# Writing TensorE's four MLP group iterations as a hardware loop instead of four copies

## The chip, the cores and the metric

The kernel runs on one core of a Trainium2 chip. The metric is the device time of one execution in microseconds (us), lower is better. The kernel before takes 1731.78 us (median of three runs, 1730.12 to 1737.38).

## The reference, cut to what matters

One inference step of a two-layer decoder trunk, with weights shared by a prompt of 512 tokens and 8 samples of one token (520 columns in all). Each layer has a mixer (differential attention with gated linear attention in layer 0, a recurrent block in layer 1), and then a squared-ReLU MLP:

```python
def sq_relu_mlp(h, w_up, w_down):
    return jnp.square(jax.nn.relu(h @ w_up)) @ w_down
...
yp = yp + rmsnorm(sq_relu_mlp(rmsnorm(yp, g[2]), w_up[layer], w_down[layer]), g[3])
```

The model width is 1024 and the MLP's inner width is 4096. The change touches only how the MLP's products are issued.

## The kernel before

All activations lie transposed: 8 tiles of 128 features by 520 tokens. Every product is done in two parts: the activation and the weight are each split into a high and a low part, and three products (high by high, low by high, high by low) are summed in PSUM. Weights arrive in chunks of 1024 rows by 256 columns (1 MB). SyncE loads a chunk into `RAW` (two slots), ScalarE copies it to `W_hi` (L699), VectorE makes `W_lo` (L1044), and TensorE multiplies it in `products` (L1525). A chunk gives two output tiles; a tile is 8 steps of 3 products by 2 halves of 260 columns, so 48 matmuls, and a chunk is 96 matmuls with as many weight loads.

The MLP of a layer is 32 chunks in four groups of eight: in a group, chunks 0 to 3 give 8 tiles of the inner layer from `H_hi`/`H_lo`, which VectorE and ScalarE turn into `U_hi`/`U_lo` (L1391, L909, L1394, L1396), and chunks 4 to 7 multiply these by the down weights, and VectorE adds the results into `ACC` (L1401). SyncE, ScalarE and VectorE already run the four groups as a hardware loop (`Fori`, at L544, L899 and L1383). TensorE's program has the four groups written out one after the other by a Python loop, in layer 0 and again in layer 1.

The engines run in order and are coupled by counting semaphores. In the MLP TensorE waits for:

- `w_lo_ready`, once per chunk (L1527), for the split weights;
- `banks_free`, once per tile (L1531), for the PSUM banks of the tile two before;
- `h_ready`, eight times in chunk 0 of a group, through `set_ready` (L1563), with the same constants in each group;
- `u_lo_ready`, eight times in chunk 4 of a group (L1575).

The values come from the class `Chunk`, which adds `g * per_group` to a constant. Where `g` is a Python integer the value is a constant in the program. Where `g` is the loop's variable, the value is in a register, worked out by register instructions on the engine that waits:

```python
at = lambda value, per_group: value if g is None else g * per_group + value
self.ready = at(c + 1, 8)
...
self.banks_free = [at(m // 2, 8) for m in self.tiles]
```

Of the kernel before, what the change touches and what calls it, by code (L numbers as in the profile page):

```python
# [114 lines left out]
def trunk(nc, ctx, a, o):  # L115
# [171 lines left out]
    def sem(name):  # L287
        return ctx.enter_context(nc.semaphore(name))
# [126 lines left out]
    u_lo_ready = sem("u_lo_ready")  # L415
# [1073 lines left out]
    def _(pe):  # L1489
# [35 lines left out]
        def products(ch, hi, lo, ready=None, after=None, together=False):  # L1525

            pe.wait_ge(w_lo_ready, ch.ready)  # L1527

            def free(i):
                if ch.tiles[i] >= 2:  # L1530
                    pe.wait_ge(banks_free[ch.par[i]], ch.banks_free[i])  # L1531

            def step(i, k):
                cols = slice(P * i, P * i + P)
                for n, (w, x) in enumerate(((W_hi, hi), (W_hi, lo), (W_lo, hi))):
                    for j, half in enumerate(halves):
                        t = MM_(PS[:, 2 * ch.par[i] + j, 0:HALF], w[:, ch.slot, k, cols], x[:, k, half],  # L1537
                                start=k == 0 and n == 0, stop=k == KT - 1 and n == 2)
                if k == KT - 1:
                    t.then_inc(tiles_done, 1)  # L1540

            if together:
                for i in range(ch.count):
                    free(i)
                for k in range(KT):
                    ready(k)
                    for i in range(ch.count):
                        step(i, k)
                if after:
                    for i in range(ch.count):  # L1550
                        after(i)
            else:
                for i in range(ch.count):
                    free(i)
                    for k in range(KT):
                        if ready and i == 0:
                            ready(k)
                        step(i, k)
                    if after:
                        after(i)  # L1560

        def set_ready(m):
            return lambda k: pe.wait_ge(h_ready, 8 * m + k + 1)  # L1563
# [3 lines left out]
                products(Chunk(c0 + j), H_hi, H_lo, set_ready(m) if j == 0 else None)  # L1567

        def mlp(layer, c0, m):
            for g in range(4):  # L1570
                for j in range(4):
                    products(Chunk(c0 + j, g), H_hi, H_lo, set_ready(m) if j == 0 else None)
                for j in range(4, 8):
                    products(Chunk(c0 + j, g), U_hi, U_lo,
                             (lambda k, g=g: pe.wait_ge(u_lo_ready, g * 8 + (32 * layer + k + 1))) if j == 4 else None)  # L1575

        sum_squares(0)

# [200 lines left out]
        sum_squares(1)  # L1779
        sum_squares(2)  # L1780
        mlp(0, C_MLP0, 2)
        sum_squares(3)
        sum_squares(4)
# [36 lines left out]
        sum_squares(5)  # L1820
        sum_squares(6)
        mlp(1, C_MLP1, 5)
        sum_squares(7)

# [53 lines left out]
```

## Time and profile before

| | |
|---|---|
| median of three runs | 1731.78 us (1730.12 to 1737.38) |
| the profiled execution: its time | 1731.78 us |
| the profiled execution: first to last instruction | 1729.9 us |
| TensorE matmuls, busy | 1494.3 us, 86% |
| VectorE, ScalarE, GpSimd, busy | 56%, 28%, 21% |
| mean granted TensorE clock | 0.893 of full speed |
| TensorE instructions | 10,928 matmuls and as many weight loads |

The profile names engines PE (TensorE's matmuls), PEld (its weight loads, which overlap the matmuls), DVE (VectorE), ACT (ScalarE), POOL (GpSimd) and SP (SyncE). A q behind a name (PEldq, ACTq, DVEq) means the engine's sequencer, that is a semaphore, register or branch instruction, which is not counted as busy time. PEclk is the granted TensorE clock. DMA queues named "instruction" carry the engines' own programs; queue q1 carries the weights.

### The profile page before, as it was taken

To read this page: it belongs to the slowest core of one execution; us is meant where nothing else is said; L and a number is where in the kernel's file an instruction comes from. 1 tells how busy PE (TensorE), PEld (TensorE's weight loads), DVE (VectorE), ACT (ScalarE), POOL (GpSimd) and SP (SyncE) were. 2 spreads that over 40 slices of the span, in tenths; PEclk is the share of its full clock that TensorE was granted. 3 is DMA by queue.
4 is the path that set the end of the run, shared out by engine and by line. 5 is a ranking of instruction groups with operands and counts; after the bars stand their busy time and mean duration, and the time that the engine had idled before them with its cause. 6 is when DMAs were issued, how large, how long until landed. Compare 5 with 4: busy or idle time off the path is not lost.

```text
span 1729.9 us, 25378 instructions
## 1 busy us (share of the span) xinstructions
PE 1494.3 (86%) x10928; PEld 1328.3 (77%) x10928; DVE 960.5 (56%) x1104; ACT 477.2 (28%) x701; POOL 358.0 (21%) x237
## 2 busy tenths in 40 slices
PE   4999636678987679799999999699897999999995
PEld 3999613346662139699999999589896999999994
DVE  3498867668866842743535353667827435343533
ACT  3322423322113112421212122346424212121222
POOL 0185756557536200200000000100302000000001
PEclk8999856768768659999999999899998999999998
DMA  8387766669668642023222332021220332233221
GB/s 285 122 302 258 257 241 239 244 245 385 243 246 348 286 147 73 27 96 98 96 83 90 98 97 84 16 75 54 94 75 25 98 98 77 95 98 98 76 71 50
DMA packets 128260, 250.54 MB, mean 145 GB/s; under 512 B 5255, under 2 KB 108699, under 8 KB 111508
## 3 DMA queue, kind: packets, MB, share of 16 engines
q0 software_dynamic: 18432, 134.23, 20.5%
q1 hardware_dynamic: 100292, 104.21, 18.8%
q10 hardware_dynamic: 9432, 10.55, 1.9%
q8 instruction: 86, 1.41, 0.3%
q14 instruction: 18, 0.15, 0.0%
HBM read 241.30 MB, written 7.73 MB: 144 GB/s over the span
## 4 chain that ended last, share of the span: by engine, by line
PE 72%; DVE 15%; ACT 5%; DMA 3%; issue 2%; SPq 2%; POOL 1%; ACTq 0%; POOLq 0%; DVEq 0%
PE PS L1537 59%; PE PS L1522 3%; PE PS L1756 2%; DVE TMP L1079 2%; DVE HRS L1312 2%; DMA SBIAS<-bias_scratch 1%; SPq L521 1%; DVE RS L1053 1%; PE PS L1669 1%; PE PS L1689 1%; DVE ST L1290 1%; PE PS L1659 1%; DVE SC L1095 1%; PE PS L1711 1%; PE PS L1795 1%
## 5 line engine op out<-in xcount | busy, mean ns | idle before, releaser
L1537 PE MATMUL PS<-H_hi,W_hi 128*128 128x260 f32 x1936 | 397.3, 287 | 23.2 <-DVE H_lo L1049 13.2
L1537 PE MATMUL PS<-H_hi,W_lo 128*128 128x260 f32 x1936 | 393.7, 285 | 0.0
L1537 PE MATMUL PS<-H_lo,W_hi 128*128 128x260 f32 x1936 | 393.5, 285 | 0.0
L1537 PEld LDWEIGHTS PS<-H_hi,W_hi 128*128 128x128 f32 x1936 | 303.9, 191 | 26.3 <-issue 19.1
L1537 PEld LDWEIGHTS PS<-H_lo,W_hi 128*128 128x128 f32 x1936 | 302.3, 191 | 0.0
L1537 PEld LDWEIGHTS PS<-H_hi,W_lo 128*128 128x128 f32 x1936 | 302.3, 191 | 0.0
L1044 DVE TENSOR_TENSOR W_lo<-RAW,W_hi 128x2048 fp32r<-128x2048 f32 x94 | 216.5, 2303 | 133.3 <-ACT W_hi L699 132.6
L699 ACT ACTIVATE W_hi<-RAW 128x2048 fp32r<-128x2048 f32 x94 | 179.5, 1909 | 278.1 <-PE PS L1537 277.7
L625 POOL TENSOR_TENSOR X<-X,TMP 128x520 f32<-128x520 f32 x16 | 26.7, 1667 | 956.9 <-DVE TMP L1079 956.9
L1537 PE MATMUL PS<-U_hi,W_lo 128*128 128x260 f32 x1024 | 206.4, 283 | 0.0
L1537 PE MATMUL PS<-U_lo,W_hi 128*128 128x260 f32 x1024 | 206.0, 283 | 0.0
L1537 PE MATMUL PS<-U_hi,W_hi 128*128 128x260 f32 x1024 | 206.0, 282 | 0.0
L578 POOL TENSOR_TENSOR PROD<-KV,QB 128x1024 f32<-128x1024 f32 x64 | 152.1, 2376 | 105.6 <-DVE SC L1095 75.1
L1537 PEld LDWEIGHTS PS<-U_hi,W_hi 128*128 128x128 f32 x1024 | 157.9, 188 | 0.0
L1537 PEld LDWEIGHTS PS<-U_hi,W_lo 128*128 128x128 f32 x1024 | 157.9, 188 | 0.0
L1537 PEld LDWEIGHTS PS<-U_lo,W_hi 128*128 128x128 f32 x1024 | 157.4, 188 | 0.0
L1401 DVE TENSOR_TENSOR ACC<-ACC,PS 128x520 f32<-128x520 f32 x64 | 44.6, 697 | 200.3 <-PE PS L1537 200.3
L909 ACT ACTIVATE UF<-SQ 128x520 f32<-128x520 f32 x64 | 40.9, 639 | 279.9 <-DVE SQ L1391 279.9
L1391 DVE SCALAR_TENSOR_TENSOR SQ<-PS,RS 128x520 f32<-128x520 f32 x64 | 44.8, 700 | 112.8 <-PE PS L1537 112.8
L1522 PE MATMUL PS<-SQ,ONES 128*128 128x260 f32 x256 | 76.0, 456 | 35.4 <-ACT SQ L721 35.4
L1689 PE MATMUL PS<-KV,PM 128*32 128x512 f32 x512 | 92.7, 821 | 8.9 <-DMA KV<-in_cache_v,CIDX 8.2
L1522 PEld LDWEIGHTS PS<-SQ,ONES 128*128 128x128 f32 x256 | 54.2, 226 | 56.0 <-issue 28.1
(284 smaller groups left out, 1612.7 us busy)
## 6 DMA issues: line engine op xcount, KB each, us to landing
RAW<-in_w_up SPq DMA_DIRECT2D x32, 1024.0 KB, 5.4
RAW<-in_w_down SPq DMA_DIRECT2D x32, 1024.0 KB, 5.1
RAW<-in_w_in_even SPq DMA_DIRECT2D x13, 1024.0 KB, 7.9
RAW<-in_w_in_odd SPq DMA_DIRECT2D x8, 1024.0 KB, 5.5
RAW<-in_w_out_odd SPq DMA_DIRECT2D x5, 1024.0 KB, 5.2
RAW<-in_w_out_even SPq DMA_DIRECT2D x4, 1024.0 KB, 6.2
x_saved<-X ACTq DMA_DIRECT2D x1, 2080.0 KB, 6.4
X<-x_saved SPq DMA_DIRECT2D x1, 2080.0 KB, 7.7
```

Source lines behind the costliest of these rows:

```text
L578: nc.gpsimd.tensor_tensor(PROD[:, 1], KV[i % RING][:, 2:4, :], QB[:, None, n // 32, :].to_broadcast([P, 2, 512]), ALU.mult).then_inc(prod1 ...
L699: A(W_hi[:, ch.slot], RAW[:, ch.slot], ACT.Copy).then_inc(w_hi_ready, 1)
L909: A(UF[:, i], RL[:, i], ACT.Square).then_inc(uf_ready, 1)
L1044: V.tensor_tensor(W_lo[:, ch.slot], RAW[:, ch.slot], W_hi[:, ch.slot].bitcast(F32), ALU.subtract).then_inc(w_lo_ready, 1)
L1079: t = V.scalar_tensor_tensor(TMP[:, q], ACC[:, kt + q], VEC[:, gain + kt + q:gain + kt + q + 1], RS[:, 1], ALU.mult, ALU.mult)
L1312: link(V.reciprocal(HRS[:, q % 2], HRS[:, q % 2]))
L1391: V.scalar_tensor_tensor(pair(RL[:, i]), banks(ch.par[i]), 0.0, pair(RS[:, 1]), ALU.max, ALU.mult).then_inc(banks_free[ch.par[i]], 1)
L1401: V.tensor_tensor(pair(ACC[:, m]), pair(ACC[:, m]), banks(ch.par[i]), ALU.add).then_inc(banks_free[ch.par[i]], 1)
L1522: t = MM_(PS[:, 4 + i, 0:HALF], ONES[:], SQ[:, kt % 2, half], start=kt == 0, stop=kt == KT - 1)
L1537: t = MM_(PS[:, 2 * ch.par[i] + j, 0:HALF], w[:, ch.slot, k, cols], x[:, k, half], start=k == 0 and n == 0, stop=k == KT - 1 and n == 2)
L1689: t = MM_(PS[32 * pos:32 * pos + 32, 6, :], PM[:, (n // 4) % 2, 4 * (n % 4) + pos].rearrange("p b j -> p (b j)"), KV[i % RING][:, pos, :], ...
L1756: t = MM_(out[:, GLA_CHUNK * n:GLA_CHUNK * n + GLA_CHUNK], ST[rows, hp, n], QE[rows, hp, P * tb + GLA_CHUNK * n:P * tb + GLA_CHUNK * (n + ...
```

## The change

`mlp` in TensorE's program runs its four groups as a hardware loop. The body is in the program once per layer and is run four times. The semaphore values that depend on the group are now held in registers.

```diff
         def mlp(layer, c0, m):
-            for g in range(4):
+            with pe.Fori(0, 4) as g:
                 for j in range(4):
                     products(Chunk(c0 + j, g), H_hi, H_lo, set_ready(m) if j == 0 else None)
                 for j in range(4, 8):
                     products(Chunk(c0 + j, g), U_hi, U_lo,
-                             (lambda k, g=g: pe.wait_ge(u_lo_ready, g * 8 + (32 * layer + k + 1))) if j == 4 else None)
+                             (lambda k: pe.wait_ge(u_lo_ready, g * 8 + (32 * layer + k + 1))) if j == 4 else None)
```

## Rows read from the trace of the kernel before

**Rows 1.** The page: busy time of each engine, share of span, instructions.
```profile
span 1729.9 us, 25378 instructions
## 1 busy us (share of the span) xinstructions
PE 1494.3 (86%) x10928; PEld 1328.3 (77%) x10928; DVE 960.5 (56%) x1104; ACT 477.2 (28%) x701; POOL 358.0 (21%) x237
```

**Rows 2.** The chain that ended last: start, length (us), what.
```profile
716.61 369.05 PE PS L1537 x3072
...
1324.67 369.07 PE PS L1537 x3072
```

**Rows 3.** Windows of layer 0's four groups: busy time (instructions), clock, DMA.
```profile
core 0: us, PE busy (x) PEld busy (x) DVE busy (x) ACT busy (x) POOL busy (x), PEclk, DMA share, GB/s
716.61:808.80 92.19, 92.19 (x769) 92.19 (x769) 41.26 (x41) 20.60 (x17) 1.02 (x1) 1.00 0.29 92
808.80:901.05 92.25, 92.25 (x770) 92.25 (x769) 38.57 (x40) 20.02 (x16) 0.00 (x0) 1.00 0.29 92
...
sum 369.04, PE 369.04 PEld 369.04 DVE 156.96 ACT 81.72 POOL 1.02; mean PE 92.26 PEld 92.26 DVE 39.24 ACT 20.43 POOL 0.26
```

**Rows 4.** Waits, 718 to 1084 us: who waited for whom, us, times, longest.
```profile
ACT UF L909 <- DVE SQ L1391: 139.9, 32, 5.1
ACT W_hi L699 <- PE PS L1537: 138.9, 15, 9.6
```

**Rows 5.** DMA queues, whole span, then 716 to 1086 us: packets, MB, share.
```profile
q8 instruction: 86, 1.41, 0.3%
q14 instruction: 18, 0.15, 0.0%
...
q8 instruction: 25, 0.41, 0.5%
q14 instruction: 2, 0.02, 0.0%
```

**Rows 6.** TensorE's semaphore instructions at L1563, 805 to 809 us.
```profile
L1563 PEldq EVENT_SEMAPHORE  x1: 51/51/51, 806.6 to 806.6; - x1
```

**Rows 7.** Timeline around 808.5 us: where the second group's matmuls begin.
```profile
808.45 0.40 PE L1537 MATMUL PS<-U_hi,W_lo 128*128 128x260 f32 x2
808.57 0.19 PEld L1537 LDWEIGHTS PS<-H_hi,W_hi 128*128 128x128 f32 x1
```

**Rows 8.** TensorE's semaphore instructions at L1563, 40 to 43 us.
```profile
L1563 PEldq EVENT_SEMAPHORE  x1: 51/51/51, 41.8 to 41.8; - x1
```

**Rows 9.** DMA queues, 42.85 to 43 us.
```profile
DMA packets 1, 0.02 MB, mean 109 GB/s; under 512 B 0, under 2 KB 0, under 8 KB 0
## 3 DMA queue, kind: packets, MB, share of 16 engines
q8 instruction: 1, 0.02, 38.8%
```

**Rows 10.** ScalarE's sequencer at its loop's end, 797 to 798 us (L899, L698).
```profile
L899 ACTq ALU_OP  x1: 35/35/35, 797.4 to 797.4; - x1
L899 ACTq COMPARE_BRANCH  x1: 67/67/67, 797.4 to 797.4; - x1
L899 ACTq FUSED_REGOPS  x1: 50/50/50, 797.6 to 797.6; - x1
...
L698 ACTq FUSED_REGOPS  x1: 37/37/37, 797.7 to 797.7; - x1
```

**Rows 11.** VectorE's sequencer at its loop (L1383), whole span.
```profile
L1383 DVEq ALU_OP  x8: 40/40/40, 808.9 to 1693.8; - x8
L1383 DVEq COMPARE_BRANCH  x8: 50/56/67, 809.0 to 1693.9; - x8
```

**Rows 12.** Timeline of VectorE: the last `U_lo` of a group, a `W_lo`.
```profile
764.71 0.70 DVE L1396 TENSOR_TENSOR U_lo<-UF,U_hi 128x520 fp32r<-128x520 f32 x1
...
810.84 2.29 DVE L1044 TENSOR_TENSOR W_lo<-RAW,W_hi 128x2048 fp32r<-128x2048 f32 x1 [1.25 <-ACT W_hi L699]
```

## The prediction, made before the changed kernel ran

> **What bounds the kernel now.** I read the page's busy times first: TensorE is busy for 1494.3 of 1729.9 us, the other engines for 56% or less [rows 1]. Then the chain of work that ended last: each layer's MLP is one unbroken piece of TensorE's matmuls, 369.05 us at 716.61 and 369.07 us at 1324.67, 3072 matmuls each [rows 2]. Together they are 738.1 us, 43% of the span, and they are all that the change touches. The windows of the four groups of layer 0 show TensorE busy for 92.19 of 92.19 us and 92.25 of 92.25 us, at granted clock 1.00 (the 2.4 GHz level) [rows 3]. Divided out, 369.05 / 3072 = 0.120 us for one weight load and matmul. In the list of waits of that stretch TensorE does not occur at all: the longest entries are ScalarE waiting for VectorE and for TensorE [rows 4]. So there is nothing in these stretches that the change could give back: no gap, full clock, the same 3072 matmuls after as before. Any effect is a cost, and the question is whether it is covered.
>
> **The change, part by part.**
>
> *What it removes.* Three of four copies of the body per layer, from TensorE's program. In layer 0's MLP, instruction queue q8 moves 25 packets, 0.41 MB, which over four groups is 6.2 packets or 0.10 MB per group; over the span q8 moves 86 packets and 1.41 MB [rows 5]. 10,928 matmuls and 10,928 weight loads [rows 1] in 1.41 MB come to 64.5 bytes each, so q8 carries TensorE's program, and a packet holds about 256 instructions. That traffic is 0.5% of the DMA engines' time in the stretch [rows 5], and TensorE never waits in it. Removing it is worth nothing.
>
> *What it adds inside the body.* Per group 32 waits get a value from a register: 8 for `w_lo_ready`, 16 for `banks_free`, 8 for `u_lo_ready`. The `h_ready` ones keep their constants. The trace of before shows no register instruction on TensorE. The nearest rows are ScalarE's, 35 to 50 ns [rows 10], and VectorE's, 40 ns [rows 11]. At 50 ns for each of 32, that is 1.6 us of sequencer time per group, spread over 92 us, and never more than three in a row (0.15 us). The cover is the sequencer's lead over the array. The semaphore instruction in front of the second group is done at 806.6 [rows 6], while the weight load behind it starts at 808.57 [rows 7]: the sequencer is 2.0 us ahead, some 17 pairs at 0.120. So 0.15 us hides. The bounds are 0 and, if nothing covers it, 8 groups x 1.6 = 13 us. I take 0, since the lead is thirteen times the longest burst.
>
> Nor does a wait that now stands in a register come due sooner. The last `U_lo` of a group ends at 764.71 + 0.70 = 765.4 [rows 12]. Its step is the eighth of the chunk that begins at 716.61 + 46.1 = 762.7, so it is due at 762.7 + 7 x 0.72 = 767.8, and 2.4 us are left. A `W_lo` made from 810.84 to 813.1 [rows 12] is for the chunk due at 808.6 + 11.5 = 820.1, with 7 us left. Behind a waiting instruction on TensorE stands only TensorE's own stream; VectorE and ScalarE wait for its tiles, and with no delay there they keep their times.
>
> *What it adds at the loop's end.* Three taken branches per layer, six in all. (The last pass falls through, and the first is entered in line.) A back-edge has a part inside the sequencer. ScalarE's loop shows it: its closing register instruction at 797.4, the branch 67 ns, and the last register instruction of the next pass's first wait at 797.7 [rows 10]. I take 0.4 us from first to last.
>
> The second part is the code. The loop's start lies 6.2 packets back, and whether it is still in the engine's instruction memory no row shows. The loops of VectorE and ScalarE took six such branches each with only 2 q14 packets in the whole stretch [rows 5], but their bodies are short: VectorE's has some 40 instructions and as many register and semaphore ones. So I bound it. The lower bound is 0: the code is there, and the 0.4 us lies inside the lead of 2.0. For the upper, the price of one fetch is read where TensorE's sequencer had been standing at a wait: its semaphore instruction is released at 41.8 [rows 8], and the next code packet runs inside 42.85 to 43.0 and on; it is alone there, filling 38.8% of 16 engines x 0.15 us = 0.93 us [rows 9]. From the release to the packet's end that is 42.9 + 0.93 - 41.8 = 2.0 us, and 2.5 when a packet takes 1.4 (25 packets at 0.5% of 16 x 370 us average 1.2). One fetch then leaves 0.4 + 2.0 to 2.5 - 2.0 = 0.4 to 0.9 us of idle array per back-edge, 2.4 to 5.4 us for six. Two fetches one after the other leave 2.4 to 3.4 us, 14 to 20 us for six. I take one fetch, at 0.65 us: 6 x 0.65 = 4 us. VectorE, ScalarE and SyncE then simply run that much later, since they wait for TensorE's tiles [rows 4].
>
> The Trainium skill has a rule on this, in "Runtime: NRT & Kernel Launch", section on instruction fetch mechanics: fetch is sequential, and a taken branch to a target outside a window of two 16 KB pages stalls until that page is fetched. That speaks against the change, and by it all six back-edges pay. The size of the code packets here agrees (1.41 MB / 86 = 16 KB). No trace so far shows a far branch.
>
> *Sum.* 0 (traffic) + 0 (registers) + 4 (six back-edges) = +4 us. Against the profiled execution, 1731.78 us with a span of 1729.9 and 1.9 around it, that is 1736; its time is also the median of the runs, so no correction is needed.
>
> **The rivals.** About 0.5% (8.7 us) is what a measurement of this kernel tells from no change.
>
> 1. *The body stays in the engine.* Then nothing is fetched at a back-edge, and 0.4 us is inside the lead of 2.0: 1732 us. For it: a memory of eight packets would hold the body's 6.2, and VectorE's and ScalarE's loops show no refetch [rows 5]. Against: q8's packets come one by one all through the unrolled stretch, so nothing shows more than the next one being kept. q8 would fall to about 86 - 6 x 6.2 = 49 packets. The Trainium skill has a rule for this too: "Advanced Engine Details and Errata", section on the ISA cache, gives TensorE 128 KB where the others have 32 KB, yet also says there are only two lines of 16 KB; by the first figure the body fits, by the second it does not.
>
> 2. *The stall is long.* A branch out of line costs more than a fetch in line: it starts with nothing in flight, or the packet behind the target is needed before it has come, or the packet queues behind weight traffic. It decides from 8.7 / 6 + 2.0 = 3.45 us per back-edge on: slower by more than 0.5%. With two fetches in a row (0.4 + 4.0 to 5.0 us) it is 14 to 20 us, and in between, with 3.5 to 4.4 us per back-edge, 9 to 14: 1741 to 1752 us. For it: nothing suggests that target and next packet come together. Against: with an empty lead the array still needs 256 x 0.06 = 15 us for a packet's instructions, so a second fetch hides unless the loop starts close to a packet's end.
>
> 3. *Register instructions are dear on TensorE.* If they had to wait until the array has drained, each of the 32 sites per group would lose the lead. At even 0.2 us each that is 8 x 32 x 0.2 = 51 us, 1783 us. Against: TensorE's semaphore instructions (51 ns) run 2.0 us ahead of the array, so the sequencer does not wait for it there [rows 6, 7].
>
> 4. *Faster.* No mechanism gives it: there is no idle time to remove [rows 3].
>
> **How the numbers follow.** My forecast (a fetch at each back-edge, 1 to 8.7 us in all) has 0.37, centred on 1736. Rival 1 has 0.30 (1732). Rival 2 has 0.26 (1741 to 1752). Rival 3 has 0.04. Faster by over 0.5% has 0.03, from noise alone. So: slower 0.26 + 0.04 = 0.30, same 0.37 + 0.30 = 0.67, faster 0.03. For the range, rival 1 less the lower spread of the runs (1732 - 2) gives about 1729, and the upper end cuts rival 2 at 2.4 us per back-edge, 1732 + 14 = 1746. What is left out is rival 3, the dear end of rival 2, and noise, under 2 in 10. The forecast's own range is 1732 to 1740.
>
> **What would show each step.** In the changed kernel's windows, TensorE should be busy without a gap inside a group at 0.120 us a pair; gaps of tens of ns at each tile would show rival 3. At the group boundaries near 808.8, 901 and 993 us there should be an idle of 0.4 to 0.9 us in the forecast, none in rival 1, over 1.5 us in rival 2. The granted clock should stay at 1.00 through them, since the array was busy until then. q8's count tells fetch from no fetch: if the body is fetched anew each pass it stays at 86 or rises by up to a packet or two per pass (86 to 98); if it stays, it falls to about 49. The prediction is wrong if the MLP stretches grow by more than 4.4 us each, or if another stage moves: the rest of TensorE's program is untouched, but its packets' boundaries shift.

## The result: 25 us slower, and all of it in one of the two loops

The changed kernel takes 1756.29 us (median of four, 1755.25 to 1759.3) against 1730.95 for the kernel before; the ratio is 1.0144, 95% interval 1.0113 to 1.0175. The forecast was 1736 us with a range of 1729 to 1746. The profiled execution took 1753.37 us, with a span of 1751.6: 21.7 us more than the profiled execution of before, and these 21.7 are what the traces below account for.

The page of the changed kernel: busy times hardly moved, the clock's mean neither, and q8 moves fewer code packets than before [rows 1, 5].

```profile
span 1751.6 us, 25540 instructions
## 1 busy us (share of the span) xinstructions
PE 1492.6 (85%) x10928; PEld 1326.9 (76%) x10928; DVE 960.4 (55%) x1104; ACT 476.5 (27%) x701; POOL 357.9 (20%) x237
...
q8 instruction: 77, 1.26, 0.3%
```

The chain that ended last answers to [rows 2] (start, length, what):

```profile
717.77 92.26 PE PS L1537 x768
...
815.35 94.78 PE PS L1537 x768
...
915.46 94.27 PE PS L1537 x768
...
1014.59 94.01 PE PS L1537 x768
...
1346.33 369.03 PE PS L1537 x3072
```

Layer 1 is still one unbroken piece of 369.03 us. Layer 0 has fallen into its four passes. Between the first and the second lie 815.35 - (717.77 + 92.26) = 5.3 us, then 5.3 and 4.9: 15.5 us of idle array. And the passes behind a gap are longer than the first, by 2.5, 2.0 and 1.8 us, 6.3 together. 15.5 + 6.3 = 21.8 us, the whole loss.

The windows around the first back-edge show what the 2.5 us are (columns as in [rows 3]):

```profile
807.60:809.90 2.30, 2.30 (x21) 2.21 (x19) 0.00 (x0) 0.00 (x0) 0.00 (x0) 1.00 0.09 20
809.90:815.30 5.40, 0.12 (x2) 0.00 (x0) 2.99 (x2) 1.91 (x1) 0.00 (x0) 0.84 0.01 3
815.30:820.30 5.00, 4.96 (x23) 4.99 (x24) 0.00 (x0) 0.00 (x0) 0.00 (x0) 0.50 0.68 213
820.30:830.00 9.70, 9.70 (x82) 9.70 (x82) 2.42 (x4) 0.64 (x1) 0.00 (x0) 0.99 0.00 0
```

In the 5 us behind the gap the granted clock is 0.50, the 1.2 GHz level, and 23 matmuls run where 42 fit at 0.120 us. Before the gap it was 1.00, and the fall came inside the gap (0.84 on average there).

TensorE's sequencer at the closing branch (L1570), whole span, then between 807 and 816 us, then the first register instruction of the next pass (L1531):

```profile
L1570 PEldq COMPARE_BRANCH  x8: 76/226/4115, 807.8 to 1713.2; - x8
...
L1570 PEldq COMPARE_BRANCH  x1: 4115/4115/4115, 807.8 to 807.8; - x1
L1570 PEldq FUSED_REGOPS  x1: 52/52/52, 812.0 to 812.0; - x1
...
L1531 PEldq ALU_OP  x1: 36/36/36, 815.1 to 815.1; - x1
```

The branch itself takes 4115 ns at 807.8. Then one register instruction runs at 812.0, and the next one in the program only at 815.1. So there are two stalls in a row, 4.1 and 3.1 us, and the array, which had 2 us of work queued, is idle from 809.9 to 815.3. The idle time is put down to no releaser:

```profile
815.31 0.50 PEld L1537 LDWEIGHTS PS<-H_hi,W_hi 128*128 128x128 f32 x2 [5.50 <-issue]
```

The code queue shows what was waited for. The rows are of 717 to 1109 us (layer 0's MLP), of 808.5 to 908.5 (one pass), of 808.5 to 811, of 811.9 to 814, and of 1345.9 to 1715 (layer 1's):

```profile
q8 instruction: 34, 0.56, 0.6%
...
q8 instruction: 9, 0.15, 0.7%
...
q8 instruction: 1, 0.02, 4.3%
...
q8 instruction: 1, 0.02, 2.8%
...
q8 instruction: 7, 0.11, 0.1%
```

Layer 0's stage fetches 34 packets where it fetched 25 before [rows 5]: seven in the first pass and nine in each pass that follows a back-edge, one of them in each of the two stalls. Layer 1's fetches seven in the whole stage, none between its first back-edge and its exit. One loop is fetched anew on each pass, the other is kept in the engine and costs nothing. Their bodies have the same length and the same instructions.

One more packet belongs to the picture. It starts just before the branch does (807.7 to 807.8 us; the branch starts at 807.83), so while the target was still to be reached, the engine had asked for one packet more:

```profile
q8 instruction: 1, 0.02, 64.8%
```

### The profile page after: what moved, and what is told of

Read it like the earlier page. It is cut to its first block, busy times and chain, and to the rows that moved or that the text cites. A ratio compares the mean times of both kernels' runs of the same rounds, so it can differ in the third digit from the quotient of the medians.

```text
span 1751.6 us, 25540 instructions
## 1 busy us (share of the span) xinstructions
PE 1492.6 (85%) x10928; PEld 1326.9 (76%) x10928; DVE 960.4 (55%) x1104; ACT 476.5 (27%) x701; POOL 357.9 (20%) x237
## 4 chain that ended last, share of the span: by engine, by line
PE 72%; DVE 15%; ACT 5%; DMA 3%; issue 2%; SPq 2%; POOL 1%; ACTq 0%; POOLq 0%; DVEq 0%
PE PS L1537 59%; PE PS L1522 3%; PE PS L1756 2%; DMA SBIAS<-bias_scratch 2%; DVE HRS L1312 2%; SPq L521 1%; PE PS L1689 1%; DVE RS L1053 1%; DVE TMP L1079 1%; PE PS L1669 1%; DVE SC L1095 1%; PE PS L1659 1%; PE PS L1795 1%; PE PS L1711 1%; DVE ST L1290 1%
```

## The experiments

The theory I formed from this (A): TensorE's instruction memory keeps eight packets of 16 KB (256 instructions), gives up the oldest for a new one, and asks for the next packet on entering one. The body has 1564 instructions in the compiled program (the trace has as many TensorE records between two closing branches), 6.1 packets. Depending on where in a packet it begins, it touches seven packets or eight. With seven, the one fetched ahead makes eight, and all stay. With eight, the one fetched ahead is the ninth, and the target is gone when the branch comes; every later packet is then pushed out just before it is needed (below, the body "thrashes"). By the two register instructions 3.1 us apart, layer 0's loop begins on the last instruction of a packet. Counting 256 at a time from there, layer 1's begins at 215 of 256: 215 + 1564 = 1779, under 7 x 256 = 1792. The rival (B): the place does not matter, and layer 0 suffers from something at its place in the kernel.

**1. Both loops at the start of a packet.** `head_slot` gives the number within a packet at which the loop's first instruction stands; the places ahead of it are filled up and jumped over.

```diff
-            with pe.Fori(0, 4) as g:
+            with nc.Fori(0, 4, engines=[pe.engine], head_slot={pe.engine: 0}) as g:
```

> The changed kernel with each of TensorE's two loops placed so that its first instruction is the first of a 16 KB code packet. Theory A (TensorE keeps eight packets, fetches one ahead, and a body that touches seven is kept whole while one that touches eight is not): both bodies of 1564 instructions, 100 KB, now touch seven packets, so no back-edge fetches, layer 0's three idle gaps of 5.2 to 5.6 us and the half-clock stretches behind them are gone, its stage is 369 us, and the time is that of the kernel before, 1731 us within noise. Theory B (layer 0's stalls come from something else at that place: the weight traffic, the other engines, being the first loop): the three gaps stay and the time is about 1756 us.

Measured: 1732.07 us, ratio to before 1.0000 (0.9982 to 1.0017). The chain has both stages whole, q8 has 50 packets, and no branch takes over 315 ns (minimum, median, maximum in ns; two of the ten are the entries):

```profile
718.36 369.05 PE PS L1537 x3072
...
1325.07 369.03 PE PS L1537 x3072
```
```profile
q8 instruction: 50, 0.82, 0.2%
```
```profile
L1570 PEldq COMPARE_BRANCH  x10: 76/215/315, 716.0 to 1691.9; - x10
```

The loop with all its register waits and branches is free. Only the place was changed, with one branch over the padding at each entry. B falls.

**2. The loop in layer 0 only** (layer 1 written out, `if layer == 0` around the loop).

> The loop in layer 0 only; layer 1's four groups are written out as before. Layer 0's loop stands where it stood in the changed kernel. If layer 0's loop carries the whole cost, as the changed kernel's trace says: three gaps of 5 to 6 us in layer 0, 369 us in layer 1, about 1756 us. If the loop in layer 1 costs something that the trace does not show as idle time, this comes out below 1753.

Measured: 1759.98 us in one execution. The four passes of layer 0 are again apart (92.24, 94.89, 94.19, 93.84 us) and layer 1 is 369.05 us. Layer 0's loop carries the whole cost.

**3. Both loops at 224 of 256**, and **4. at 232**: the same edit with `224` and `232`.

> As the run with the loops at the start of a packet, but at instruction 224 of 256. 224 + 1564 = 1788, four short of seven packets (1792). Theory A: still seven packets, no gap at any back-edge, 1731 us. If it were closeness of the loop's start to a packet's end that costs (the packet behind the target needed too early), 32 instructions are left before the next one and gaps should show: 2 us or more for each of six.

> The same at instruction 232 of 256. 232 + 1564 = 1796, four over seven packets. Theory A: eight packets, both loops thrash: all six back-edges wait for the target packet and then for the next one, which is needed 24 instructions later; 4 to 5.6 us idle each and 2 us of half clock, so +36 to +46 us: 1767 to 1777. Theory B, in which the place does not matter: as the changed kernel, 1756. Code packets on q8 rise by nine per pass in both layers.

Measured: 1733.42 us at 224 and 1761.81 us at 232, one execution each. At 224 all back-edges take 0.2 us. One gap of 1.2 us is at layer 0's entry, where the loop is now reached by a branch over padding and the packet behind its start is needed 32 instructions later. At 232 the chain shows layer 1 in pieces, and layer 0 broken at its first back-edge alone:

```profile
722.63 91.21 PE PS L1537 x758
818.70 276.07 PE PS L1537 x2294
...
1334.27 92.27 PE PS L1537 x768
...
1431.98 93.58 PE PS L1537 x758
...
1530.85 93.62 PE PS L1537 x758
...
1630.46 93.34 PE PS L1537 x758
```

Eight instructions of displacement, 224 to 232, turn no stall into four, as the theory says of the limit of 1792. But I expected six. In layer 0 the first pass asked for a ninth packet, at 811.5, and its back-edge stalled. The second pass fetched eight packets and not nine, the ninth was not asked for before its branch at 908.1, and the last two passes fetched none. So the stall comes and goes with the ninth packet. At 232 the body ends only four instructions into its eighth packet. That this was too short to ask for the ninth each time is a guess.

**5. Both loops at 239**, eleven over the limit.

> Both loops at instruction 239 of 256: 239 + 1564 = 1803, eleven over seven packets. At 232, four over, layer 0 stalled at its first back-edge only. Theory A with a race (four instructions are too few for the next packet to be asked for each time): now both layers thrash at all three back-edges: nine packets per pass, gaps of 4 to 5.6 us, six in all, +36 to +45 us, 1767 to 1776. If layer 0's later passes hit again, the rule of eight packets is not the whole of it.

Measured: 1775.62 us, one execution. q8 has 105 packets, and both layers are broken at all three back-edges:

```profile
L1570 PEldq COMPARE_BRANCH  x10: 79/3924/4101, 718.7 to 1735.5; - x10
```
```profile
q8 instruction: 105, 1.72, 0.4%
```

Here each back-edge has two shorter gaps (2.28 and 1.04 us at the first), since 17 instructions of the target packet can be issued before the next packet is needed. Seven matmuls with their weight loads run between the two gaps, ten at 232: that is what 17 and 24 instructions hold, and it confirms the places. So every place tried at least eleven over the limit stalls each time, and every place tried under it never does.

**6. The loop in layer 1 only.**

> The loop in layer 1 only; layer 0 written out. Its start lies at the same place of a packet as in the changed kernel, 172 in the program's count, and there it was kept whole. Theory A: no gap in either layer, 369 us each, 1731 us within noise: half of the change is free where the place is right. If the loop in layer 1 was free only because layer 0's had run before it, it now shows three gaps and 1750 or more.

Measured: 1731.08 us, one execution; stages of 369.07 and 369.05 us, and no q8 packet between 1414 and 1690 us. Half of the change is free, by the luck of its place.

**7. One instruction more ahead of layer 0's loop.**

```diff
         def mlp(layer, c0, m):
+            if layer == 0:
+                pe.wait_ge(ones_set, 1)
+                pe.wait_ge(root_ready, 1)
+                pe.wait_ge(x_loaded, 16)
             with pe.Fori(0, 4) as g:
```

> The changed kernel with waits ahead of layer 0's loop that have long been met; they add one semaphore instruction to TensorE's program and nothing else. The changed kernel's trace reads as if layer 0's loop began on the last instruction of a packet (its first instruction runs when the target packet has come, the second 3.1 us later, when the next one has). Theory A: one instruction further the loop begins on a packet's first instruction, its body touches seven packets, all three stalls go, layer 1 stays whole (216 + 1564 is below 1792), and the time is 1731 us instead of 1756. If the start is not where I read it, or the place of the loop is not the cause, the three gaps of 5.5 us stay, 1756.

Measured: 1733.80 us, ratio 1.0007 (0.9989 to 1.0025), q8 with 50 packets, stages of 369.12 and 369.07 us, and no branch over 248 ns:

```profile
L1574 PEldq COMPARE_BRANCH  x8: 76/208/248, 807.3 to 1692.0; - x8
```

The three waits are one semaphore instruction in the compiled program (the trace has 144 of them ahead of the loop and had 143), and that one instruction takes away 23 us.

**8. A body of two groups**, run twice, at the start of a packet: 3127 instructions, 12.2 packets, more than can be kept.

```diff
-            with pe.Fori(0, 4) as g:
-                ...
+            with nc.Fori(0, 2, engines=[pe.engine], head_slot={pe.engine: 0}) as h:
+                group(h * 2)
+                group(h * 2 + 1)
```

> Each layer's loop has two passes of two groups, so a body of 3127 instructions, twelve packets, which fits in no memory of eight; it begins at the start of a packet. Theory A: one far back-edge per layer. The branch waits for its target packet (4.1 us in the changed kernel), the packet behind it is needed only 256 instructions later and is hidden, so idle is 4.1 + 0.3 - 2.0 = 2.4 us per layer: one gap of 2.4 to 2.8 us in each stage, and 0 to 2 us more each if the clock falls: +5 to +9 us, 1738 to 1742. If the two serial fetches of the changed kernel belong to every far branch, wherever the loop begins, the gap is 5.5 us and the sum +11 to +16.

Measured: 1741.77 us, ratio 1.0047 (1.0030 to 1.0064), that is +8.1 us for two far branches (branches whose target is no longer in the engine). This is a far branch by itself. The windows of layer 0's back-edge:

```profile
724.00:910.10 186.10, 186.10 (x1540) 185.72 (x1539) 80.21 (x81) 40.59 (x33) 1.43 (x1) 1.00 0.30 91
910.10:912.80 2.70, 0.26 (x3) 0.08 (x2) 1.19 (x2) 1.91 (x1) 0.00 (x0) 1.00 0.00 0
912.80:918.00 5.20, 5.20 (x31) 5.20 (x32) 1.80 (x1) 0.00 (x0) 0.00 (x0) 0.67 0.38 97
```

The branch takes 4.2 us, the array is idle for 2.4 (4.2 + 0.3 - 2.0 gives 2.5), and a stretch at reduced clock follows: 31 matmuls where 43 fit. In the chain the second half of each stage is 186.29 us where the first is 184.6, so the clock costs 1.7 us and a far branch 4.1 in all. The second fetch does not belong to every far branch.

**9. The prefetch hint**, an instruction at the top of each pass that announces the closing branch, at the changed kernel's own place, **10.** at 239, and **11.** on the body of two groups.

```diff
-            with pe.Fori(0, 4) as g:
+            with nc.Fori(0, 4, engines=[pe.engine], hint_back_edge=True) as g:
```

> The changed kernel with a prefetch hint for the closing branch, given at the top of every pass; one instruction more in the body, the same place. If the hint makes the target packet be there when the branch comes, the branch takes 0.2 us instead of 4.1, and only the wait for the packet behind the target is left: gaps in layer 0 of 1 to 3 us instead of 5.5, +4 to +10 us, 1736 to 1742. If a hint given 92 us ahead fetches a packet that is pushed out again before the branch, nothing changes: 1756. Layer 1 fits as before and stays at 369 us.

> Both loops at instruction 239, where each back-edge stalled (1775.6 us without the hint), now with the prefetch hint. In the run with the hint at the changed kernel's own place the stalls went, but the hint is itself an instruction and that loop began on a packet's last one, so either the hint or the shift can have done it. If the hint does it: branches of 0.2 us at 239 too, no gap above 1 us or only the one for the packet behind the target (1.5 to 2 us), 1731 to 1745. If it was the shift: branches of 4 us, gaps of 2.5 and 1.9 us, about 1775 us as without the hint.

> The body of two groups, twelve packets, with the hint. Without it each layer paid one branch of 4.1 to 4.2 us, a gap of 2.5 us and 4.2 us in all (1741.8 us, +8). A body of this size can't be kept, so only an early fetch can help. If the hint fetches the target in time: branches of 0.2 us, no gap, 1732 us. If what it fetches at the top of the pass is pushed out before the branch: as without it, 1741 us.

Measured: 1740.52 us in one execution for the first, with both stages at 369.05 and 369.07 us and no long branch. It proves nothing by itself, since the hint is an instruction more in the body and experiment 7 showed what one instruction does. Its 8 us over before lie ahead of the stages: layer 0's begins at 724.98 instead of 716.61, and from there to layer 1's it is 608.0 us, as before. At 239 the hint gives 1733.50 us, ratio 1.0015 (1.0000 to 1.0031), where the same place without it gave 1775.62:

```profile
L1570 PEldq COMPARE_BRANCH  x10: 80/216/323, 714.8 to 1691.2; - x10
```
```profile
q8 instruction: 51, 0.84, 0.2%
```

So the hint does it. The count says how: 51 packets are the body fetched once. With the hint the ninth packet is not fetched, the eight stay, and nothing is pushed out. It also shows that distance alone is not the cause: the target lies seven packets back, just as it did at 239 without the hint, and the branch takes 0.22 us. On the body that cannot be kept (1734.93 us, ratio 1.0024, 1.0010 to 1.0037) the branch still takes 2.4 us instead of 4.2:

```profile
L1577 PEldq COMPARE_BRANCH  x1: 2412/2412/2412, 899.9 to 899.9; - x1
```

Most of that is inside the lead. The second half of a stage begins at 902.80, where the first ended at 717.57 + 184.54 = 902.11, so 0.7 us are idle, and the clock does not fall:

```profile
717.57 184.54 PE PS L1537 x1536
902.80 184.77 PE PS L1537 x1536
```

The hint stands at the top of the pass, 184 us ahead, but no extra fetch follows there. One packet starts between 899.8 and 899.9, as the branch does at 899.9. Without the hint two start around the branch of 908.1, one between 908.2 and 908.3 and one between 909.1 and 909.2. It looks as if the hint made the engine ask for the target where it would have asked for the next packet in order: about 1 us sooner than the branch itself, which is not enough to hide it. In experiments 9 and 10 the target is still there, so nothing at all is asked for. That reading fits all three runs; no run tests it by itself. I had expected all of it or none.

No version here is faster than the kernel before.

## Why the prediction was wrong, step by step

- *Nothing to gain, the loop's registers free:* right. With the places right, the loop with its register waits measures 1.0000 and 1.0007 of before, and q8 falls to 50 packets, where rival 1 said 49. The rival of dear register instructions is refuted.
- *The lead of 2.0 us covers the branch's own work:* right. Branches in memory take 0.21 to 0.25 us. In the stalls the array worked on from 807.8 to 809.9.
- *Whether the code is still there:* I gave "stays" and "is fetched" one answer for both loops. The trace of before could not tell, and both occurred: layer 1 went the way of the first rival, layer 0 that of the second. What I lacked is that the place decides. The 25 packets that come one by one through the unrolled stretch [rows 5] I counted against rival 1; they say only that code which runs on is fetched one ahead, not that what is behind is dropped.
- *"I take one fetch, at 0.65 us: 6 x 0.65 = 4 us":* this is the step that failed, in both its factors: three back-edges paid and not six, and each paid 7.3 us and not 0.65. The price of a fetch was read to the packet's end, 2.0 to 2.5 us, but the engine goes on only 1.4 us later: branch at 807.8, its packet started at 808.8 and was 4.3% x 16 x 2.5 = 1.7 us long, next instruction at 812.0. A far branch measured 3.7 to 4.1 us in layer 0 and 4.1 to 4.2 in experiment 8. The lead took 2.0 of it, and 2.3 to 2.4 us idle are left (experiment 8), not 0.65. And there were two fetches one after the other, since the loop begins on a packet's last instruction. I had that as the dear bound (2.4 to 3.4 us; the gaps measured 4.9 to 5.3) and argued against it as needing a start "close to a packet's end". It had just that.
- *"The granted clock should stay at 1.00":* wrong. Behind 5.3 us of idle array it was 0.50 for 5 us, behind 2.4 us it was 0.67 on average over 5.2. That is 1.7 to 2.5 us per back-edge which the sum lacked.
- *The sum:* forecast 6 x 0.65 = 4 us. Measured in the trace: 15.5 idle + 6.3 clock = 21.8 for three back-edges of layer 0, and 0 for three of layer 1. Rival 2 with two fetches in a row had 14 to 20 us for six branches without the clock; it was three branches, dearer ones, with it, and the time came out above rival 2's upper end of 1752 too.
- The Trainium skill's rule in "Runtime: NRT & Kernel Launch" (instruction fetch mechanics), that a taken branch outside a window of two pages forces a fetch, is borne out by layer 0 and refuted by layer 1, where the target lies six packets back and the branch takes 0.2 us. The Trainium skill's "Advanced Engine Details and Errata" (ISA cache) gives TensorE 128 KB, which agrees with eight packets of 16 KB; the two cache lines that it gives in the same place do not.

Open: why layer 0 at 232 did not ask for the ninth packet in its second pass, and where exactly between 224 and 239 the limit lies. The order in which packets are given up is argued from the count of nine per pass, and no run shows it directly. Experiments 2 to 6 and 9 are one execution each; the differences of 27 to 44 us in 2, 4 and 5 are far outside the spread of a kernel's executions (up to 15 us from lowest to highest), the 8 us in 9 are not.

## What to carry to other kernels

Rolling this long stretch of TensorE code into a hardware loop removed nothing that the array waited for, and cost 4 to 7 us at each back-edge that stalled. Before doing so, count the body in packets of 256 instructions and where it begins. Here seven packets touched never stalled at a back-edge, eight stalled each time at 239 and at 255 of 256 (the changed kernel's layer 0), and so did the body of 12.2 packets. If it must be a loop, pin its start or give the back-edge a hint, and look at the branch's duration (0.2 or 4 us here) and at the code queue's count in the profile. This kernel moved by 23 us when one instruction was added ahead of its loop. By the same count it should do so for one added anywhere earlier in TensorE's program (not run), and an edit elsewhere would then seem to have done what only the shift did.

## What the runs showed of the hardware that I had not expected

- Two loops of the same 1564 instructions, one refetched at nine packets a pass, the other kept for three passes without one.
- A far branch on TensorE takes 3.7 to 4.1 us in the changed kernel (4115 ns at the first, of which the packet's transfer is 1.7 us); a taken branch in memory takes 0.21 to 0.25 (experiment 1), one that falls through 0.08.
- An idle array of 2.4 us was enough to bring the clock down: the 5 us behind it ran at 0.67 on average, and behind 5.3 us at 0.50. Gaps of 1.2 us (experiment 3) and 0.7 us (experiment 11) left it at 1.00.
- The hint keeps a body of eight packets whole; the instruction takes 31 to 41 ns (experiment 10).
